# Two output projections and two FFN down-projections finished chunk by chunk, with the tokens kept in four-group order

## The reference

```python
def rms_norm(x, g):
    xf = x.astype(jnp.float32)
    y = xf * lax.rsqrt(jnp.mean(xf * xf, axis=-1, keepdims=True) + NORM_EPS)
    return (y * g.astype(jnp.float32)).astype(x.dtype)
...
    return o @ w_out, new_rows                     # end of attn_mixer
...
    out = ((yn + bonus.reshape(Bt, T, D)) * g.astype(jnp.float32)).astype(h.dtype) @ w_o   # end of rwkv7_mixer
...
    y = (jax.nn.gelu(gate, approximate=True) * val) @ w_down                               # end of conv_ffn
```

## Time and profile before

| | us |
|---|---|
| median of 3 runs (4934.9 to 4941.7) | 4935.95 |
| span of the profiled execution | 4937.4 |
| PE busy in it | 4283.9 (87%) |
| DVE busy | 2783.5 (56%) |
| ACT busy | 1081.8 (22%) |
| POOL busy | 319.0 (6%) |
| mean granted TensorE clock | 0.928 of full speed |

### The profile page before, as it was taken

The page is one execution under the profiler, slowest core; times in us unless marked ns, Lnnn a source line. Parts: engine busy times, 40 slices in busy tenths (PEclk is TensorE's granted clock), DMA queues, the critical chain, the costliest instruction groups (busy, mean ns, idle before and its releaser), DMA issues. The chain is left out here.

```text
span 4937.4 us, 82552 instructions
## 1 busy us (share of the span) xinstructions
PE 4283.9 (87%) x33016; PEld 3158.5 (64%) x33016; DVE 2783.5 (56%) x3905; ACT 1081.8 (22%) x1979; POOL 319.0 (6%) x443
## 2 busy tenths in 40 slices
PE   8997989877767789999996999688886969999997
PEld 5565335444434478887993655377784548888896
DVE  4798665289921355555335122479986155555444
ACT  1200554344431112222001011122222012222100
POOL 0000000400054000000000000122220000000000
PEclk9998999899978899999997999799997979999998
DMA  3012000399965211112442231422213211111343
GB/s 101 22 39 64 1 1 1 89 345 348 363 192 155 70 34 42 42 42 59 118 118 90 70 111 65 156 62 56 62 34 154 73 63 39 40 42 52 103 116 119
DMA packets 539511, 463.29 MB, mean 94 GB/s; under 512 B 77602, under 2 KB 453962, under 8 KB 534747
## 3 DMA queue, kind: packets, MB, share of 16 engines
q1 hardware_dynamic: 508386, 409.36, 26.2%
q10 hardware_dynamic: 21088, 32.80, 2.0%
q0 software_dynamic: 9728, 16.80, 1.2%
HBM read 397.01 MB, written 61.71 MB: 93 GB/s over the span
## 5 line engine op out<-in xcount | busy, mean ns | idle before, releaser
L313 PE MATMUL proj_acc<-hT,oT 128*128 128x352 f32 x864 | 258.4, 462 | 6.2 <-SPq L287 6.2
L2440 PE MATMUL fdown_acc<-hidden,oT 128*128 128x176 f32 x1584 | 248.3, 316 | 0.0
L2440 PEld LDWEIGHTS fdown_acc<-hidden,oT 128*128 128x128 f32 x1584 | 242.8, 193 | 0.7 <-issue 0.5
L313 PEld LDWEIGHTS proj_acc<-hT,oT 128*128 128x128 f32 x864 | 165.4, 192 | 99.5 <-SPq L287 7.1
L2184 PE MATMUL fup_acc_a<-h,w_up_first 128*128 128x264 f32 x704 | 169.7, 396 | 50.8 <-ACTq L2217 50.8
L2184 PEld LDWEIGHTS fup_acc_a<-h,w_up_first 128*128 128x128 f32 x704 | 137.5, 196 | 77.4 <-ACTq L2217 52.9
L517 DVE TENSOR_SCALAR_CACHE_REDUCE oT<-scores,proj_cand 128x384 bf16<-128x384 f32 (+1 forms) x186 | 164.4, 943 | 1.1
L2184 PE MATMUL fup_acc_c<-h,oT 128*128 128x264 f32 x704 | 163.8, 386 | 0.0
L2184 PE MATMUL fup_acc_d<-oT 128*128 128x264 f32 x704 | 163.8, 386 | 0.0
L2184 PE MATMUL fup_acc_b<-oT 128*128 128x264 f32 x704 | 163.8, 386 | 0.0
L2184 PE MATMUL fup_acc_d<-h,oT 128*128 128x264 f32 x704 | 163.8, 386 | 0.0
(11 more groups left out here) (645 smaller groups left out, 8608.0 us busy)
## 6 DMA issues: line engine op xcount, KB each, us to landing
oT<-in_ffn_w_down SPq DMA_DIRECT2D x96, 704.0 KB, 4.5
fup_w<-in_ffn_w_up SPq DMA_DIRECT2D x66, 512.0 KB, 4.9
scores<-in_cache_sb_k SPq DMA_DIRECT2D x128, 256.0 KB, 5.8
qb<-in_cache_sb_k SPq DMA_DIRECT2D x128, 256.0 KB, 6.2
qi<-in_cache_sb_v SPq DMA_DIRECT2D x128, 256.0 KB, 5.8
ka<-in_cache_sb_v SPq DMA_DIRECT2D x128, 256.0 KB, 6.3
w_up_first<-in_ffn_w_up SPq DMA_DIRECT2D x22, 512.0 KB, 3.8
x_between<-oT SPq DMA_DIRECT2D x16, 528.0 KB, 2.7
```

The lines of the kernel that those rows point to most:

```text
L313: last = pe.matmul(acc[u][0:m, c, 0:CW], w[u][:, k, 0:m], hT[:, k, c * CW:(c + 1) * CW], start=(k == 0), stop=(k == KD - 1))
L2440: last = pe.matmul(bank[n], weights[:, k, :], moving[:, k, :], start=begin and k == 0, stop=k == DOWN_K - 1, skip_group_check=True)
```

## The change

All of x, from the first stage on, is kept in the order of four groups (256 prompt tokens, 8 new tokens, four times), so that no stage has to reorder it before the FFN. The new helpers `tile_cols`, `batch_cols`, `grouped` and `spread_groups` give the columns. Code that wrote tiles of 128 tokens to x writes them to the new columns; RWKV still works in plain order, so `stage_rwkv_vectors` and `stage_rwkv_out` each use two instructions (1024 and 32 tokens) where one of 1056 stood, and `stage_y` first packs the 32 new tokens.

`stage_out` is rewritten. All eight weight tiles are resident, the loop is chunk by chunk (24 units of 8 matmuls), and the closing work of chunk c-1 stands between the units of chunk c. The ones matrix is used with all 128 columns, so the root comes out on all partitions and nothing has to be spread. The stage also makes `h` itself, scaled by gain and root. `stage_ffn_up` loses its 24 scaling instructions. `stage_ffn_down` closes chunk c-1 between the steps of chunk c in the same way; the old residual is fetched by chunk into `hidden`, which is free by then.

```diff
+            for u, (c, n) in enumerate(units):
+                if c == 0:
+                    pe.wait_ge(w_loaded[n], 16 * n_loads)
+                if u >= RING:
+                    pe.wait_ge(taken, u - RING + 1)
                 for k in range(KD):
+                    last = pe.matmul(acc[:, u % RING, 0:CW], w[n][:, k, :], src[:, k, cols(c)], start=k == 0, stop=k == KD - 1)
                 last.then_inc(product, 1)
+                if u >= 1:
+                    sums(u - 1)
+                if c >= 1 and n == 5:
+                    sums_new(c - 1)
+            sums(len(units) - 1)
+            pe.wait_ge(taken, len(units))
+            taps.turn(pe, K, acc)
+            sums_new(NCH - 1)
...
+            for u, (c, n) in enumerate(units):
+                dve.wait_ge(product, u + 1)
+                dve.tensor_copy(dst[:, n, cols(c)], acc[:, u % RING, 0:CW]).then_inc(taken, 1)
...
+                if c >= 1 and n == 2:
+                    renew(c - 1)
+                if c >= 1 and n == 7:
+                    norm(c - 1)
+            renew(NCH - 1)
+            norm(NCH - 1)
...
-            for k in range(HK):
-                scale_half(k, 0)
-                scale_samples(k)
-            for k in range(HK):
-                scale_half(k, 1)
-            for k in range(HK, KD):
-                scale_half(k, 0)
-                scale_half(k, 1)
-                scale_samples(k)
-            dve.wait_ge(scaled, 3 * KD)
-            dve.wait_ge(saved, 16 * KD)
+            dve.wait_ge(saved, 16 * NCH)
...
             def sums(m):
-                c = STEPS[m][0]
+                c, q = STEPS[m]
+                if q == 0 and c >= 1:
+                    pe.wait_ge(rooted, c)
                 for i in range(2):
                     pe.wait_ge(squared, 2 * m + i + 1)
+                    pe.matmul(power[:, 0:CW], K.ones[:, :], square[:, i, :], start=q == 0 and i == 0, stop=q == QUADS - 1 and i == 1)\
+                      .then_inc(summed, 1)
...
+                if gain_next is not None and c >= 1 and q == QUADS - 1:
+                    sums_new(c - 1)
...
+            if gain_next is not None:
+                norm(0)
+                norm(1)
+            invert(NCH - 1)
+            scale(NCH - 1, range(QUADS + 1))
+            add(NCH - 1, 0)
+            scale(NCH - 1, range(QUADS + 1, KD))
+            add(NCH - 1, 1)
+            if gain_next is not None:
+                norm(NCH - 1)
```

More of the change, by code:

```diff
@@ L1955, in store, with stage_out @@
             act.dma_start(self.out_s.rearrange("b w n -> (b w) n")[:, at], self.rows[i][2:18, :]).then_inc(self.stored, 16)
-def stage_out(nc, K, name, src, kt, loads, dst, x_in, x_out, gain, gain_next, fetch=None, first=None, taps=None, follow=(), save=None):
+def stage_out(nc, K, name, src, loads, dst, x, x_old, gain, gain_next, first, first_here, taps, follow, save):
+    RING, SQUARES = 4, 3
+    units = [(c, n) for c in range(NCH) for n in range(KD)]
     with Stage(nc, name) as s:
-        w = [first if u == 0 and first is not None else s.sb(f"w{u}", [P, kt, P]) for u in range(2)]
-        square = s.sb("square", [P, 2, T])
-        inverse = [s.sb(f"inverse{i}", [P, CW]) for i in range(2)]
+        w = [first] + [s.sb(f"w{n}", [P, KD, P]) for n in range(1, KD)]
+        xin = s.sb("xin", [P, KD, T])
+        square = s.sb("square", [P, SQUARES, CW])
+        inverse, again = K.rstd[:, 0:CW], K.rstd[:, CW:2 * CW]
@@ L1994, in _ @@
-                if n == 2 and fetch is not None:
-                    sp.dma_start(x_in[:, :, :], fetch).then_inc(fetched, 16)
-            if follow:
-                sp.wait_ge(product, KD - 1)
-                for dst_w, dram in follow:
-                    sp.dma_start(dst_w, dram).then_inc(followed, 16)
-                sp.wait_ge(followed, 16 * len(follow))
-            sp.wait_ge(gained, 16 if gain_next is None else 32)
-            if save is not None:
-                for k in range(KD):
-                    sp.wait_ge(added, k + 1)
-                    sp.dma_start(save[0][:, k, :], x_out[:, k, :]).then_inc(save[1], 16)
+                        sp.dma_start(K.gain[:, :], gain_next.rearrange("(k p) -> p k", p=P)).then_inc(gained, 16)
@@ new lines, in _ @@
+            for c in range(NCH):
+                sp.dma_start(xin[:, :, cols(c)], x_old[:, :, cols(c)]).then_inc(fetched[c], 16)
+            taps.load(sp)
+            sp.wait_ge(gained, 32)
+            for c in range(NCH):
+                sp.wait_ge(added, 2 * c + 2)
+                sp.dma_start(save[0][:, :, cols(c)], x[:, :, cols(c)]).then_inc(save[1], 16)
+                if c == NCH - 1:
+                    sp.wait_ge(product, NCH * KD)
+                    for dst_w, dram in follow:
+                        sp.dma_start(dst_w, dram).then_inc(followed, 16)
@@ L2007, in _ @@
+            sp.wait_ge(followed, 16 * len(follow))
         @block.tensor
         def _(pe):
-            for bank in power:
-                pe.matmul(bank[:, :], K.zeros16[:, 0:P], K.zeros16[:, :], start=True, stop=False, skip_group_check=True)
-            def sums(i, n):
-                pe.wait_ge(squared, KD * i + n + 1)
-                for c in range(NCH):
-                    last = pe.matmul(power[i][32 * c:32 * c + 32, 0:CW], K.ones[:, 0:32], square[:, n % 2, c * CW:(c + 1) * CW], start=False,
-                                     stop=(n == KD - 1), skip_group_check=True)
-                last.then_inc(summed, 1)
@@ L2036, in _, with sums @@
-            sums(0, KD - 1)
-            pe.wait_ge(taken, KD)
-            spread_rows(0)
-            if taps:
-                taps.turn(pe, K, acc[1])
-            if gain_next is not None:
-                for k in range(KD):
-                    sums(1, k)
-                if taps:
-                    pe.wait_ge(taps.taken, 1)
-                spread_rows(1)
+            def sums(u):
+                c, n = units[u]
+                pe.wait_ge(squared, u + 1)
+                if n == 0 and c >= 2:
+                    pe.wait_ge(rooted, c - 1)
+                pe.matmul(power[c % 2][:, 0:CW], K.ones[:, :], square[:, u % SQUARES, :], start=n == 0, stop=n == KD - 1).then_inc(summed, 1)
@@ L2067, in _ @@
+            root(NCH - 1)
+            taps.take(act, acc)
+            squares_new(NCH - 1)
+            root_new(NCH - 1)
         @block.vector
         def _(dve):
-            for n in range(KD):
-                dve.wait_ge(product, n + 1)
-                dve.tensor_copy(row3(dst[:, n, :]), chunks(acc[n % 2])).then_inc(taken, 1)
-            dve.wait_ge(rooted, 1)
-            dve.reciprocal(inverse[0][0:96, :], inverse[0][0:96, :]).then_inc(inverted, 1)
-            dve.wait_ge(taken, KD)
@@ L2075, in _ @@
-            dve.wait_ge(gained, 16 if gain_next is None else 32)
-            if fetch is not None:
-                dve.wait_ge(fetched, 16)
-            dve.wait_ge(spread, 1)
-            def add(k):
-                dve.wait_ge(scaled, k + 1)
-                dve.tensor_tensor(x_out[:, k, :], x_in[:, k, :], dst[:, k, :], ALU.add).then_inc(added, 1)
-            for k in range(KD):
-                dve.scalar_tensor_tensor(out=row3(dst[:, k, :]), in0=row3(dst[:, k, :]), scalar=gcol[:, k:k + 1], in1=chunks(acc[0]),
-                                         op0=ALU.mult, op1=ALU.mult).then_inc(scaled, 1)
-                if k >= 1:
-                    add(k - 1)
-                if k == 4 and taps:
-                    taps.take(dve, acc[1])
@@ L2407, in _, with fetch @@
         def _(sp):
+            def fetch(c):
+                sp.wait_ge(product, 7 * QUADS * (c + 1))
+                sp.dma_start(old_x(c), x_saved[:, :, chunk(c)]).then_inc(fetched[c], 16)
             for i in range(4):
@@ L2434, in _ @@
         def _(pe):
-            for b in power:
-                pe.matmul(b[:, :], K.zeros16[:, 0:P], K.zeros16[:, :], start=True, stop=False, skip_group_check=True)
             def multiply(n, weights, moving, begin):
```

391 lines of the change are left out of this document (224 added, 167 removed).

## The result

| | before | after |
|---|---|---|
| median, us | 4937.56 (4 runs, 4934.9 to 4941.7) | 4916.44 (4 runs, 4913.65 to 4919.24) |
| ratio | 1 | 0.9956, 95% interval 0.9945 to 0.9968 |
| span of the profiled execution | 4937.4 | 4914.5 |
| mean granted clock | 0.928 | 0.935 |

The change makes the kernel 0.44% faster, 21 us by the medians and 22.9 by the two profiled spans. The forecast was 4923. I read the gain stretch by stretch, each from the first or last instruction of its kind in the timelines ("loop": a stage's first product to its last copy or evacuation; "closing": from there to the next stage's first matmul, or for the first `fdown` to its first DVE instruction, for the second to `stage_y`'s first transpose).

What follows compares the result with a forecast made beforehand. PE bounds the loops; uncovered closings are one chain over DVE, ACT and PE, DVE longest. Terms 2.4 - 2.0 - 15.7 + 1.1 = -14.2, rounded to -13: 4936 - 13 = 4923 us, 8 in 10 from 4909 to 4940.

Steps and rivals of the forecast that it cites:

- PE in `stage_out`: Projection loops: full-width sums at 0.63 us each on a full PE make each loop 138.2 us, 19 longer.
- rival 1: Full-width sums in projections and `fdown` cost 0.93 us, not 0.63: 4939, or 4931 with half; chance 0.16 in either size.
- The hold-up behind `renew`: `stage_out` loop: PE's sum of unit n=3 waits for a square behind `renew`, 0.6 us twice, 1.2 per stage.
- The count of 119.2 for the old loop: Old `stage_out` loop up to the last product: 8 x 14.2 + 6 x 0.93 = 119.2 us.
- The closing of `stage_out`: From the last product to `fup`'s first matmul: 44.0 us in place of 61.5, 17.5 gained.
- The first `fdown`: Loop: 16 sums +9.5, cheaper step sums -1.5; closing 24.3 us against 35.4, -11.1; with `stage_rwkv_vectors` +1.1, sum -2.0.
- The change of form: `fdown` steps: full-width sums take 1.27 us where two sums and the switch between forms took 1.41, -1.5 per stage.
- The second `fdown`: Closing up to `stage_y` 13.2 us in place of 27.4, -14.2, and -1.5 for the sums: -15.7, the main gain.
- The vectors: Split instructions cost +1.1 in `stage_rwkv_vectors` and +1.1 in `stage_rwkv_out`; `ro` gets 0.6 back from dropped matmuls on zeros.
- The late weights (4): `stage_out`, chunk 0: resident weight tiles come too late and PE waits; 4973 at 9 us per tile; chance 0.05.
- uncovered closing work (5): Closing work in the loop isn't covered, since PE waits in order for sums: 4939; chance 0.09 with other stalls.
- rivals 2 and 3: Closings: clock not given back, late sums at 1.17 us each, 4929, chance 0.12; or clock holds, 4917, chance 0.08.

Runs made afterwards that it cites:

- the changed kernel again: The changed kernel run once more with nothing altered, as the mark for the runs beside it, against the kernel before: 4917.25 us, ratio 0.9952.

## Why the prediction was right, and where it was off

The direction and the main account held, and the likeliest value was 6.6 us too high: a gain of 13 us was forecast and 21 measured. Its terms gave 14.2, and the rounding to 13 for hand-overs went the wrong way. In its own order:

- **PE in `stage_out`.** The sum costs 0.60 between products; 0.63 was taken, and rival 1's 0.93 is out. The hold-up behind `renew` is 0.7 us (one sum in `aout` starts at 1630.27, 0.6 later than the rhythm asks), with 0.6 forecast. The loops are 17.4 and 19.4 longer, with 19.0 forecast. The count of 119.2 for the old loop leaves out its slow start: the earlier trace rows has 122.0. The low clock at the start costs `aout` 2.8 us before and 1.6 after, and `ro` 1.5 before and 2.4 after. So 17.4 and 19.4 are some 18.6 and 18.5 without it, and how near each is to 19.0 is in part the clock's luck.
- **The closing of `stage_out`.** 44.3 and 42.9 us, with 44.0 forecast, and its steps are where the text put them: `norm(1)` in front of the reciprocal (6.8 us after the last copy, 7.0 forecast), late sums 7.9 and 6.6 (7.3), the weight tile 1.87 (2). That `norm(1)` costs is shown by the run with it behind, though at some 3 us each and not the 4.6 expected there. The agreement to 0.3 us in `aout` is in part luck: the same code takes 42.7 to 44.4 us by what the clock does in the late sums.
- **The first `fdown`: here a step failed.** "PE gets 16 sums in the loop, +9.5". In the code `sums_new(c - 1)` stands behind the last multiplication of the step q=3, and for chunk 1 that is the very last product. Only eight sums (4.7) lie in the loop; the other eight lie in the closing, ahead of the sums of the last step. So the root starts 5.9 us behind the last evacuation, and the reciprocal at 7.6 and not at 5.1. The loop was +1.3 and not +8.0, the closing -8.7 and not -11.1: 4.3 us better in sum (2.8 in the changed kernel again, where the loop is +3.0 and the closing -8.9). That a misread order made the forecast too high and not too low is luck. The run with the other order bears out the second half of this: the closing loses 4.3 us when the last step's sums go first and `norm(0)` and `norm(1)` last.
- **The change of form was under-sized.** Two full sums save 0.23 in a step and not 0.14: 11 steps make -2.5 where -1.5 was put, and the loop of the second `fdown` came out -3.2. The run with narrow sums agrees, with +2.3 and +2.5, though a loop can't be read finer than 1.5 to 2 us.
- **Forgotten.** The matmuls on zeros at the start of both `fdown`s (0.8 each) go as well; they stood ahead of the first product, and so are in the -1.9 and -0.6 of the `fup` rows. The rest of the -1.9 is the clock, which came back 1.2 us sooner in `fup` 0's first multiplication (5.62 in place of 6.79) and 0.2 later in `fup` 1's.
- **The second `fdown`.** 13.16 with 13.2 forecast, and 13.16 again in the repeated run. The fetch was no wait.
- **The vectors.** +1.8 with +1.6 forecast shows nothing: the stretch differs by 5.6 us between executions of the same code.
- **The rivals.** The late weights (4) and the uncovered closing work (5) don't occur: the first chunk's units are as far apart as the later ones, and PE's only rests in the loop are the two hold-ups. The clock is given back in the late sums but late (between rivals 2 and 3): 7.9, 7.15 and 6.6 us. In rival 4 the text reads the earlier trace rows as three loads issued together; the row is one DMA of 4.2 MB. The 1.7 us per tile follows from it all the same.
- **The chances.** With a third of the forecast's 0.5 given to "same", 0.33 is left for "faster", where the text has 0.36.

What the gain is made of is shown, not only argued, for the projections (old form put back: 6 us less in these stages), for `norm(1)`, the order at the end of the first `fdown` (sums and DVE's part together) and the width of the sums. That the closings of the two `fdown`s carry the gain is read from the table of stretches and from the run with the old `stage_out`, which keeps both the gain and the short closings; `stage_ffn_down` was not put back by itself.

## What to carry to other kernels

Closing work that is moved between the products costs PE its full price where PE sets the loop, so move what belongs to DVE and ACT into the loop and leave PE's part in the closing. Here it cost nothing there, and the eight sums behind it ran at the full clock. In an in-order queue look at the very last step of a loop: what was written as "behind the step" stands there in front of the chain that ends the stage. And when a prologue gets its data ready-made, look again at the credits that hold the first matmul: here two of them were worth as much as the whole rewrite.

## What the runs showed of the hardware

- Between full-width products, three sums on a quarter of the array's columns cost 0.93 us together, one such sum alone 0.91, and one on all columns 0.60. Paid for is the change of form, some 0.3 us there and back, and not the number of narrow sums.
- In the first `fdown` the granted clock fell to 0.50 at the end of a rest of 3.94 us; with matmuls of no use in most of that rest it stayed at 1.00, in both runs that have them. The 44 small transposes in the closing of a projection did not keep it: in the three runs that have eight sums directly behind them, these took 5.00 us once and 6.57 to 6.70 five times, in the same code. The late sums of the changed kernel's order take 6.6 to 8.0. What the low clock costs a stretch therefore varies by more than 1 us between executions of one kernel.
- A DVE scaling costs 1.24 us for 1056 tokens and 0.50 for 352, so cutting it in three costs a fifth more. A reciprocal of 352 tokens costs 2.35, as much as nearly five such scalings.
